# Fourier mixing in two halves of channels, and both head pairs of linear attention in one loop

## The chip, the cores and the metric

The kernel runs on one core of one Trainium2 chip. The metric is the device time of one execution in microseconds (us); the median of three runs of the kernel before is 4420.57.

## The reference

Two blocks follow each other on 2048 tokens of width 1024, all in float32. The first has two layers; each normalises and modulates the tokens (and 256 context tokens), projects them, and mixes three ways. The two ways that the change touches:

```python
def fourier_mix(u, w_four):        # u: (B, L, 256), four groups of 64 channels
    ug = u.reshape(B, L, 4, 64)
    f = jnp.fft.fft2(ug, axes=(1, 3), norm="ortho").real
    return f.reshape(B, L, 256) @ w_four

def gla_scan(q, k, v, log_a, s0):  # 4 heads, dk 48, dv 96, chunks of 64 tokens
    def step(state, inp):
        b = jnp.cumsum(gi, axis=2); b_end = b[:, :, -1:, :]
        q_dec = qi * jnp.exp(b); k_dec = ki * jnp.exp(-b)
        a = jnp.where(tri, q_dec @ k_dec.T, 0.0)
        o = a @ vi + q_dec @ state
        state = jnp.exp(b_end) * state + (ki * jnp.exp(b_end - b)).T @ vi
        return state, o
```

The scan runs forward and backward, each from the state that the context tokens leave, and the two outputs are added. The third way, neighbourhood attention with a table of biases, stands between the two. In layer 1 the context tokens need no outputs. The second block (attention, a gated MLP, embeddings) is not touched.

## The kernel before

Everything is a chain of stages. A stage is a `Block` with a program for each engine; engines wait for each other by semaphores inside it, and all meet at its end. For each layer of the first block the stages are: channel-major projection, token-major projection, Fourier (`fourier_phase`), neighbourhood attention (`neighbourhood_phase`), linear attention (`gla_phase`), output projection (`out_phase`). SP issues most DMAs from one hardware queue in program order, GpSimd ("POOL") others from its own.

**`fourier_phase`, lines 1100 to 1239.** The 2048-point transform over positions is split 128 x 16, and the transform over channels is folded with `w_four` into one 256x512 matrix `w2` (cosine and sine part). First step (L1180 to L1186): for each of 16 residues of position, and in layer 0 for the two context tiles, `ab[t] = x[t] w2`, evacuated by VectorE (L1222) and ScalarE (L1234) in turn. Second step (L1190 to L1197): for each residue four matmuls of 256 columns with the DFT table `d1` give 512 values, evacuated by ScalarE into one of four buffers `yo` (L1239) and stored by SP to the scratch `four_y` (L1141). After each of the first eight stores SP also issues six loads of bias rows (`load_near`, L1057, 48 in all). Then `four_y` is read back transposed into `ab` by four loads (L1148), which wait for all stores. Third step: for each of 16 tiles two matmuls of 256 columns with `d2` (L1205, L1206), and in layer 0 the context products with `dc` (L1210); VectorE evacuates into three buffers `fo` (L1228), GpSimd stores them (L1162, L1164) and waits for the last to land before the stage ends. The biases for the next stage are prepared here: the pad (L1031) and its copy to memory (L1035) are issued by SP, which waits for the first before it issues the lines, queries and keys (L1042 to L1047); VectorE builds the first tables (L1082, L1088) between the first step's and the third step's evacuations.

**`gla_phase`, lines 1504 to 1808.** The heads go in two pairs, `hh` 0 and 1. For each pair: the decayed keys times the decay to the chunk's end (`keys_to_end`, L1700) are transposed on TensorE and evacuated by ScalarE (L1591, L1780); batches of five chunks per direction form `k^T v` (`states`, L1613), which VectorE chains into states (`chain`, L1724: ten updates to a batch, seven batches of 35 steps); then a loop over tiles of 128 tokens, 18 in layer 0 and 16 in layer 1: scores (`products`, L1630), mask and sum of both directions (`masked`, L1734, L1737), scores times values (`inside`, L1649), queries times states (`outputs`, L1664), evacuation by ScalarE (L1789), store by SP (L1574). In each pass four batches are chained before the loop, and three in its first three tiles. The decay products of the second pair are made by VectorE in tiles 3 to 8 of the first pass (L1696, L1700, L1707), the transposes in tiles 6 and 8. Both passes share one array of states, so the second pair's chain starts after the first pass. In the second pass ScalarE and GpSimd also split the output weights into high and low parts (L1915, L1920), with the eight rows loaded by SP at its start (L1902).

```python
for hh in range(2):
    for i in range(4):
        chain(hh, i)
    for n in range(NO):
        masked(hh * NO + n)
        if n < 3:
            chain(hh, 4 + n)
        elif hh == 0:
            prepare(n - 3)
```

Of the kernel before, what the change touches and what calls it, by code (L numbers as in the profile page):

```python
# [8 lines left out]
I32 = mybir.dt.int32  # L9
# [1001 lines left out]
class Neighbourhood:  # L1011


    def __init__(self, P, last):
# [12 lines left out]
        self.lines_in, self.mask_ok, self.table_ok = P.sem("lines_in"), P.sem("mask_ok"), P.sem("table_ok")  # L1027

# [71 lines left out]
def fourier_phase(nc, l, io, keep, na):  # L1100
# [4 lines left out]
    with phase(nc, f"four{l}") as P:  # L1105
# [6 lines left out]
        dc = P.sb("dc", [128, 2, 2, 256])  # L1112
        ab = P.sb("ab", [128, N2 + 2, 512])
        yo = [P.sb(f"yo{j}", [128, 512]) for j in range(4)]
        fo = [P.sb(f"fo{j}", [128, 256]) for j in range(3)]
# [5 lines left out]
        yi_in = [P.sem(f"yi_in{j}") for j in range(4)]  # L1121
        o_out = [P.sem(f"o_out{j}") for j in range(3)]
        NAB = N2 if na.last else N2 + 2
        LF = LX if na.last else LT
        yrows = io["four_y"].rearrange("(p t) c -> p t c", t=N2)
        NO = 16 if na.last else 16 + 2
        with nc.Block() as block:
            @block.sync
            def _(sp):
# [14 lines left out]
                for j in range(4):  # L1144
                    sp.wait_ge(y_out[j], 16 * (N2 // 4))
                sp.wait_ge(y_mm, N2)
                for j in range(4):
                    sp.dma_start(ab[:, 4 * j:4 * j + 4, :],  # L1148
                                 io["four_y"][j * 512:(j + 1) * 512, :].rearrange("(a p) c -> p a c", p=128)).then_inc(yi_in[j], 16)

            @block.gpsimd
            def _(pool):
                na.clear(nc, pool)
                pool.wait_ge(na.q_in, 16)
                for i in range(3):
                    na.queries(nc, i)
                for n in range(NO):
                    pool.wait_ge(o_ev, n + 1)
                    if n < 16:

                        dst = io["mix"][0:LX, 0:256].rearrange("(a b c) d -> b a c d", a=16, b=16)[n, :, :, :]
                        pool.dma_start(dst, fo[n % 3][:, :]).then_inc(o_out[n % 3], 16)  # L1162
                    else:
                        pool.dma_start(io["mix"][LX + (n - 16) * 128:LX + (n - 15) * 128, 0:256],  # L1164
                                       fo[n % 3][:, :]).then_inc(o_out[n % 3], 16)
                for j in range(3):
                    pool.wait_ge(o_out[j], 16 * ((NO + 2 - j) // 3))

            @block.tensor
            def _(pe):  # L1170
# [9 lines left out]
                for t in range(NAB):  # L1180
# [5 lines left out]
                    last.then_inc(ab_mm, 1)  # L1186
                pe.wait_ge(d1_in, 16)
                pe.wait_ge(ab_dve, NAB // 2)
                pe.wait_ge(ab_act, NAB // 2)
                for t in range(N2):  # L1190
                    if t >= 2:
                        pe.wait_ge(y_ev, t - 1)
                    b = acc[4 + t % 2]
                    nc.tensor.matmul(b[:, 0:256], d1[:, t, 0, :], ab[:, t, 0:256], start=True, stop=False)
                    nc.tensor.matmul(b[:, 0:256], d1[:, t, 2, :], ab[:, t, 256:512], start=False, stop=True)
# [3 lines left out]
                for n in range(NO):  # L1199
                    if n >= 2:  # L1200
                        pe.wait_ge(o_ev, n - 1)
# [14 lines left out]
            def _(dve):  # L1216
# [7 lines left out]
                for n in range(NO):  # L1224
                    dve.wait_ge(o_mm, n + 1)
                    if n >= 3:
                        dve.wait_ge(o_out[n % 3], 16 * (n // 3))
# [2057 lines left out]
```

## Time and profile before

| | us |
|---|---|
| median of three runs (4420.44 to 4422.55) | 4420.57 |
| the profiled execution | 4425.12 |
| its span | 4423.3 |
| busy in it: TensorE matmuls / weight loads | 3993.2 / 3242.6 |
| busy in it: VectorE / ScalarE / GpSimd | 2073.9 / 1431.5 / 600.5 |
| mean granted TensorE clock | 0.947 |

The profile covers one execution; its span is the time from its first to its last instruction, and the sum of what the engines do can be read only against it. Matmuls are pipelined, so records of a stream overlap; the distance from start to start is what one costs. A float32 matmul has two records.

### The profile page before, as it was taken

To read this page: it belongs to the slowest core of one execution; us is meant where nothing else is said; L and a number is where in the kernel's file an instruction comes from. 1 tells how busy PE (TensorE), PEld (TensorE's weight loads), DVE (VectorE), ACT (ScalarE), POOL (GpSimd) and SP (SyncE) were. 2 spreads that over 40 slices of the span, in tenths; PEclk is the share of its full clock that TensorE was granted. 3 is DMA by queue.
4 is the path that set the end of the run, shared out by engine and by line. 5 is a ranking of instruction groups with operands and counts; after the bars stand their busy time and mean duration, and the time that the engine had idled before them with its cause. 6 is when DMAs were issued, how large, how long until landed. Compare 5 with 4: busy or idle time off the path is not lost. (4 is left out here: it accounts for less than half of the span.)

```text
span 4423.3 us, 65778 instructions
## 1 busy us (share of the span) xinstructions
PE 3993.2 (90%) x24975; PEld 3242.6 (73%) x24975; DVE 2073.9 (47%) x4599; ACT 1431.5 (32%) x3255; POOL 600.5 (14%) x669
## 2 busy tenths in 40 slices
PE   7999999799669799999979858979999989979799
PEld 4777789577558688778857647858778767768687
DVE  5364111167666542111117666732770357657554
ACT  5001344156322320144316522421111467721211
POOL 3021000033010120000012210021440001000100
PEclk8999999999779899999999979989999989979899
DMA  5244221631245432222262235441121133357221
GB/s 191 88 154 138 79 76 62 231 117 58 99 163 217 185 107 72 94 74 80 85 210 104 79 113 194 181 158 72 58 90 67 46 122 107 100 195 264 81 81 62
DMA packets 235562, 525.84 MB, mean 119 GB/s; under 512 B 55118, under 2 KB 105762, under 8 KB 225906
## 3 DMA queue, kind: packets, MB, share of 16 engines
q1 hardware_dynamic: 211634, 440.59, 28.1%
q0 software_dynamic: 23616, 81.06, 5.0%
q8 instruction: 200, 3.28, 0.3%
q14 instruction: 112, 0.92, 0.1%
HBM read 330.43 MB, written 191.13 MB: 118 GB/s over the span
## 5 line engine op out<-in xcount | busy, mean ns | idle before, releaser
L72 PE MATMUL tm_tacc<-tm_tw_hi,hT_hi 128*128 128x384 f32 (+1 forms) x1120 | 414.0, 370 | 17.9 <-DVE tm_tw_lo L906 9.6
L73 PE MATMUL tm_tacc<-tm_tw_lo,hT_hi 128*128 128x384 f32 (+1 forms) x1120 | 409.8, 366 | 0.0
L74 PE MATMUL tm_tacc<-tm_tw_hi,hT_lo 128*128 128x384 f32 (+1 forms) x1120 | 409.7, 366 | 0.0
L72 PE MATMUL tz_tacc<-tz_tw_hi,hT_hi 128*128 128x512 f32 x896 | 359.3, 401 | 5.9 <-POOL tz_tw_lo L935 3.9
L72 PE MATMUL cm_acc<-hT_hi,cm_wb_hi 128*128 128x512 f32 (+1 forms) x912 | 362.0, 397 | 0.0
L73 PE MATMUL tz_tacc<-tz_tw_lo,hT_hi 128*128 128x512 f32 x896 | 355.1, 396 | 0.0
L74 PE MATMUL tz_tacc<-tz_tw_hi,hT_lo 128*128 128x512 f32 x896 | 355.0, 396 | 0.0
L74 PE MATMUL cm_acc<-hT_hi,cm_wb_lo 128*128 128x512 f32 (+1 forms) x912 | 344.2, 377 | 0.0
L73 PE MATMUL cm_acc<-hT_lo,cm_wb_hi 128*128 128x512 f32 (+1 forms) x912 | 344.0, 377 | 0.0
L788 DVE SCALAR_TENSOR_TENSOR tm_ds<-tm_dg,tm_ds 128x512 f32<-128x512 f32 (+1 forms) x40 | 25.6, 639 | 533.2 <-ACT tm_ds L782 533.2
L72 PEld LDWEIGHTS tm_tacc<-tm_tw_hi,hT_hi 128*128 128x128 f32 x1120 | 210.6, 188 | 60.2 <-DVE tm_tw_lo L906 13.9
L74 PEld LDWEIGHTS tm_tacc<-tm_tw_hi,hT_lo 128*128 128x128 f32 x1120 | 210.8, 188 | 25.1
L73 PEld LDWEIGHTS tm_tacc<-tm_tw_lo,hT_hi 128*128 128x128 f32 x1120 | 211.0, 188 | 23.8
L72 PE MATMUL out_acc<-wo_hi,out_mT_hi 128*128 128x512 f32 x544 | 219.0, 403 | 0.0
L73 PE MATMUL out_acc<-wo_lo,out_mT_hi 128*128 128x512 f32 x544 | 215.3, 396 | 0.0
L74 PE MATMUL out_acc<-wo_hi,out_mT_lo 128*128 128x512 f32 x544 | 213.3, 392 | 0.0
L967 ACT ACTIVATE tm_tz<-tm_tacc 128x384 f32<-128x384 f32 (+1 forms) x140 | 75.6, 540 | 411.2 <-PE tm_tacc L74 410.2
L72 PEld LDWEIGHTS tz_tacc<-tz_tw_hi,hT_hi 128*128 128x128 f32 x896 | 168.9, 189 | 52.4 <-POOL tz_tw_lo L935 7.4
L704 ACT ACTIVATE cm_zo<-cm_acc 128x512 f32<-128x512 f32 (+1 forms) x57 | 32.1, 564 | 536.6 <-PE cm_acc L74 536.6
L72 PEld LDWEIGHTS cm_acc<-hT_hi,cm_wb_hi 128*128 128x128 f32 x912 | 173.3, 190 | 42.1 <-issue 12.0
L73 PEld LDWEIGHTS cm_acc<-hT_lo,cm_wb_hi 128*128 128x128 f32 x912 | 173.2, 190 | 38.0 <-issue 7.7
L74 PEld LDWEIGHTS tz_tacc<-tz_tw_hi,hT_lo 128*128 128x128 f32 x896 | 168.9, 189 | 41.1
(382 smaller groups left out, 8675.6 us busy)
## 6 DMA issues: line engine op xcount, KB each, us to landing
scr_z<-tz_tz SPq DMA_DIRECT2D x112, 256.0 KB
scr_zcm<-cm_zo SPq DMA_DIRECT2D x96, 256.0 KB, 2.0
scr_ztm<-tm_tz SPq DMA_DIRECT2D x68, 256.0 KB, 2.0
scr_xres<-out_x POOLq DMA_DIRECT2D x34, 512.0 KB, 4.1
cm_area<-in_w_ada POOLq DMA_DIRECT2D x64, 256.0 KB, 3.0
scr_z<-out_xn POOLq DMA_DIRECT2D x32, 512.0 KB, 4.7
mo_z<-scr_z SPq DMA_DIRECT2D x16, 1024.0 KB, 5.8
tz_traw<-in_w_in SPq DMA_DIRECT2D x7, 2048.0 KB, 9.1
```

The costliest lines, as they stand in the source:

```text
L72: nc.tensor.matmul(out, ah, bh, start=start, stop=False)
L73: nc.tensor.matmul(out, ah, bl, start=False, stop=False)
L74: return nc.tensor.matmul(out, al, bh, start=False, stop=stop)
L704: act.activation(zo[n % 4][:, 0:b - a], acc[n % 4][:, 0:b - a], ACT.Copy).then_inc(ev_act, 1)
L788: nc.vector.scalar_tensor_tensor(s, g, 0.0, s, ALU.min, ALU.subtract)
L967: act.activation(zo[n % 3][:, 0:widths[c]], acc[n % 3][:, 0:widths[c]], funcs[c]).then_inc(ev, 1)
```

## The change

Fourier: the second step works on one half of the channels at a time. A pass of eight units makes two residues each with 128-column matmuls; after ten of the sixteen units SP issues the first half's read-back, after the last the second's. The columns of `w2` are reordered so that each half has its cosine and sine part together. The context tiles' first and last steps move between the second and the third step. The third step fills one 512-wide bank with four tiles of a half; outputs go to one array `fo` for all tiles, stored by SP and GpSimd in turn, and their landing is waited for by SP in neighbourhood attention, at its third tile. The pad, its copy and the 48 loads of bias rows go to GpSimd's queue, ahead of its query products.

Linear attention: the second pair has its own states (in the arrays of keys and queries that are free by then, and one more). Its key products are made by GpSimd from the start, its query products by VectorE in eight pieces in tiles 3, 4, 5, 7 and 9, its transposes in tiles 3 and 4; its seven batches of states are formed after tiles 5, 7, ..., 17 and chained by VectorE one iteration later. The mask of tile g+1 goes ahead of what VectorE does for tile g. The mask itself becomes one multiplication by 0, 1 or 2 and two predicated copies of 64 columns. Values are loaded in three parts, keys scaled in five pieces, outputs have four buffers, the output weights are loaded row by row, and the high parts start at tile 3 of the second pass.

The core of the diff:

```diff
+    def four_stored(self, eng):
+        eng.wait_ge(self.four_sp, 16 * (NX // 2))
+        eng.wait_ge(self.four_pool, 16 * (NX // 2 if self.last else NT - NX // 2))
...
-                na.load_bias(sp, l, io)
                 na.load_lines(sp, io)
                 na.load_tokens(sp, io)
-                for t in range(N2):
-                    sp.wait_ge(y_ev, t + 1)
-                    sp.dma_start(yrows[:, t, :], yo[t % 4][:, :]).then_inc(y_out[t % 4], 16)
-                    if t < QR:
-                        na.load_near(sp, io, t)
...
+                for i in range(2 * NY):
+                    sp.wait_ge(y_ev, i + 1)
+                    sp.dma_start(ystore[i // NY, :, i % NY, :], yo[i % 4][:, :]).then_inc(y_out[i % 4], 16)
+                    if i == NY + 1:
+                        load_y(0)
+                load_y(1)
+                for n in range(1, NX, 2):
+                    sp.wait_ge(o_ev, first + 5 + n // 4)
+                    sp.dma_start(mix[n, :, :, :], fo[:, n, :]).then_inc(na.four_sp, 16)
...
                 na.clear(nc, pool)
+                na.load_bias(pool, l, io)
+                for r in range(QR):
+                    na.load_near(pool, io, r)
                 pool.wait_ge(na.q_in, 16)
...
+                    for x in range(2):
+                        t = 2 * u + x
+                        re, im = ab[:, t, 256 * h:256 * h + 128], ab[:, t, 256 * h + 128:256 * h + 256]
+                        b = acc[4 + i % 2][:, 256 * x:256 * x + 256]
+                        nc.tensor.matmul(b[:, 0:128], d1[:, t, 0, :], re, start=True, stop=False)
+                        nc.tensor.matmul(b[:, 0:128], d1[:, t, 2, :], im, start=False, stop=True)
+                        nc.tensor.matmul(b[:, 128:256], d1[:, t, 1, :], re, start=True, stop=False)
+                        last = nc.tensor.matmul(b[:, 128:256], d1[:, t, 0, :], im, start=False, stop=True)
...
+        build = {5 + 2 * i: i for i in range(NB)}
+        pieces = {3: (0, 1), 4: (2, 3), 5: (4, 5), 7: (6,), 9: (7,)}
...
+                masked(0)
+                for g in range(2 * NO):
+                    if g + 1 < 2 * NO:
+                        masked(g + 1)
+                    if g < 3:
+                        chain(0, 4 + g)
+                    for j in pieces.get(g, ()):
+                        queries_decayed(j)
...
+                    if g - 1 in build:
+                        chain(1, build[g - 1])
...
             def _(pool):
+                for d in range(2):
+                    pool.wait_ge(m["exp_k"], d + 1)
+                    pool.wait_ge(k_in, 16)
+                    nc.gpsimd.tensor_tensor(kd[1][d][:, :], k[:, :], kd[1][d][:, :], ALU.mult).then_inc(m["kd_ok"], 1)
...
-                    if n == KC // 2:
+                    if n == 3:
                         act.wait_ge(m["u_mm"], 2 * NB)
-                    if n < KC:
-                        wo.high(act, n)
+                    if 3 <= n < KC + 3:
+                        wo.high(act, n - 3)
```

## Rows read from the trace of the kernel before

**Rows 1.** Windows, core 0: stretch, us, busy time (instructions) by engine, granted clock, DMA.
```profile
1137.40:1276.70 139.30, 82.65 (x2072) 72.02 (x2072) 90.83 (x259) 40.69 (x106) 20.34 (x16) 0.75 0.36 126
1205.90:1218.30 12.40, 8.11 (x264) 6.80 (x264) 4.74 (x19) 2.74 (x14) 0.00 (x0) 1.00 0.19 58
1234.50:1249.00 14.50, 8.36 (x200) 7.33 (x200) 11.72 (x40) 4.00 (x9) 6.43 (x6) 0.62 0.08 25
2200.50:2313.50 113.00, 80.86 (x272) 60.54 (x272) 18.57 (x34) 14.33 (x25) 12.18 (x21) 0.91 0.67 230
2532.10:2667.90 135.80, 76.80 (x1912) 67.54 (x1912) 86.91 (x247) 38.33 (x99) 20.30 (x16) 0.75 0.36 126
```

**Rows 2.** Timeline, Fourier stage of layer 0: start, us, what [idle before, releaser].
```profile
798.52 31.24 PE L1185 MATMUL four_acc<-four_w,four_fx 128*128 128x512 f32 x72 [2.35 <-DMA four_fx<-scr_zcm]
...
830.54 0.67 PE L1194 MATMUL four_acc<-four_ab,four_d 128*128 128x256 f32 x2 [0.78 <-ACT four_ab L1234]
...
847.40 2.93 SPq L1057 DMA_DIRECT2D nain_near<-scr_rpb_pad  x6
...
863.29 3.60 DVE L1088 TENSOR_TENSOR nain_tab<-nain_near,nain_mask 128x496 f32<-128x496 f32 x6
...
867.63 0.60 ACT L1239 ACTIVATE four_yo<-four_acc 128x512 f32<-128x512 f32 x1 [1.13 <-PE four_acc L1197]
870.36 2.29 SPq L1148 DMA_DIRECT2D four_ab<-scr_four_y  x4
876.05 1.19 PE L1205 MATMUL four_acc<-four_ab,four_d 128*128 128x256 f32 x2 [8.46 <-DMA four_ab<-scr_four_y]
...
901.23 0.42 DVE L1228 COPY four_fo<-four_acc 128x256 f32<-128x256 f32 x1 [1.30 <-PE four_acc L1210]
...
906.76 0.76 PE L1347 MATMUL na_sp<-nain_k,nain_qt 64*128 64x256 f32 x1 [5.57 <-PEq L79]
```

**Rows 3.** Groups by line, whole span: count, busy, mean ns, idle before, releasers.
```profile
L1194 PE MATMUL four_acc<-four_ab,four_d 128*128 128x256 f32 x64 | 20.4, 401 | 17.7 <-ACT four_yo L1239 16.2 <-ACT four_ab L1234 1.6
L1205 PE MATMUL four_acc<-four_ab,four_d 128*128 128x256 f32 x64 | 23.0, 445 | 23.4 <-DMA four_ab<-scr_four_y 17.7 <-DVE four_fo L1228 5.4
```

**Rows 4.** Timeline, TensorE in the second block's mixing stage.
```profile
4057.21 1.05 PE L2729 MATMUL mo_SG<-mo_z,mo_wsT 128*128 128x128 f32 x8
4058.11 0.60 PE L2738 MATMUL mo_TD<-ident,mo_mx 128*128 128x128 f32 x4
```

**Rows 5.** Groups by line, GpSimd, whole span.
```profile
L1920 POOL TENSOR_TENSOR wo_lo<-wo_row,wo_hi 128x512 fp32r<-128x512 f32 x32 | 40.6, 1299 | 283.8 <-ACT wo_hi L1915 283.8
L1162 POOL DMA_DIRECT2D scr_mix<-four_fo x32 | 17.2, 536 | 124.8 <-DVE four_fo L1228 124.2 <-issue 0.7
```

**Rows 6.** Timeline, Fourier stage of layer 1, start of the second step.
```profile
2241.29 0.67 PE L1194 MATMUL four_acc<-four_ab,four_d 128*128 128x256 f32 x2 [0.78 <-ACT four_ab L1234]
```

**Rows 7.** DMA issues: count, KB each, median us to landing.
```profile
nain_k<-scr_zcm SPq DMA_DIRECT2D x2, 3456.0 KB, 18.4
```

**Rows 8.** Timeline, linear attention of layer 0.
```profile
1137.51 5.03 DVE L1700 TENSOR_TENSOR gla_kd<-nain_row,nain_eb 128x2304 f32<-128x2304 f32 x2 [3.76 <-PEq L79]
...
1149.64 4.82 PE L1613 MATMUL gla_bank<-gla_v,wo_kt 64*64 64x96 f32 x160 [2.75 <-DMA gla_v<-scr_ztm]
1151.66 13.05 DVE L1724 SCALAR_TENSOR_TENSOR gla_S<-gla_S,nain_eb,gla_bank 128x96 f32<-128x96 f32 x40 [8.63 <-PE gla_bank L1613]
...
1164.82 0.50 DVE L1734 COPY_PREDICATED gla_at<-gla_mask,gla_bank 128x128 f32<-128x128 int32 x2
1165.40 0.29 DVE L1737 TENSOR_TENSOR gla_asum<-gla_at 128x128 f32<-128x128 f32 x1
...
1191.79 4.29 PE L1591 MATMUL gla_bank<-ident,wo_ke 128*128 128x128 f32 x18
...
1220.42 13.05 DVE L1724 SCALAR_TENSOR_TENSOR gla_S<-gla_S,nain_eb,gla_bank 128x96 f32<-128x96 f32 x40 [3.89 <-PE gla_bank L1613]
...
1238.56 0.91 DVE L1737 TENSOR_TENSOR gla_asum<-gla_at 128x128 f32<-128x128 f32 x1
```

More of the change, by code:

```diff
@@ L1120, in fourier_phase @@
         y_out = [P.sem(f"y_out{j}") for j in range(4)]
[L1121 to L1126, printed above, removed]
+        yi_in = [[P.sem(f"yi_in{h}{j}") for j in range(4)] for h in range(2)]
+        NY = N2 // 2
+        ystore = io["four_y"].rearrange("(h p u) c -> h p u c", h=2, u=NY)
+        yload = io["four_y"].rearrange("(h r) (x c) -> h (r x) c", h=2, x=2)
+        first = 0 if na.last else 1
+        NO = first + 8
+        mix = io["mix"][0:LX, 0:256].rearrange("(a b c) d -> b a c d", a=16, b=16)
         with nc.Block() as block:
@@ L1179, in _, with channels @@
                 pe.wait_ge(fx_in, 16)
-                for t in range(NAB):
+                def channels(t):
                     if t >= 2:
@@ L1186, in _ @@
                     last.then_inc(ab_mm, 1)
-                pe.wait_ge(d1_in, 16)
[L1188 to L1195, printed above, removed]
-                    nc.tensor.matmul(b[:, 256:512], d1[:, t, 1, :], ab[:, t, 0:256], start=True, stop=False)
-                    nc.tensor.matmul(b[:, 256:512], d1[:, t, 0, :], ab[:, t, 256:512], start=False, stop=True).then_inc(y_mm, 1)
@@ new lines, in _ @@
+                for t in range(N2):
+                    channels(t)
+                pe.wait_ge(d1_in, 16)
+                pe.wait_ge(ab_dve, N2 // 2)
+                pe.wait_ge(ab_act, N2 // 2)
+                for i in range(2 * NY):
+                    h, u = i // NY, i % NY
+                    if i >= 2:
+                        pe.wait_ge(y_ev, i - 1)
+                    for x in range(2):
[6 more added lines that the diff above has]
+                        last = nc.tensor.matmul(b[:, 128:256], d1[:, t, 0, :], im, start=False, stop=True)
+                    last.then_inc(y_mm, 1)
@@ new lines, in _ @@
+                for j in range(8):
+                    h, b = j // 4, ready(first + j)
+                    pe.wait_ge(yi_in[h][j % 4], 16)
+                    for x in range(4):
+                        n = 4 * (j % 4) + x
+                        nc.tensor.matmul(b[:, 128 * x:128 * x + 128], d2[:, 0, :], ab[:, n, 256 * h:256 * h + 128], start=True, stop=False)
+                        last = nc.tensor.matmul(b[:, 128 * x:128 * x + 128], d2[:, 1, :], ab[:, n, 256 * h + 128:256 * h + 256], start=False, stop=True)
@@ L1514, in gla_phase @@
         mask = P.sb("mask", [128, 2, CH], I32)
+        twice, after, flat = P.sb("twice", [128, CH]), P.sb("after", [128, CH]), P.sb("flat", [128, 2, CH])
         ls = pre.ls
@@ L1691, in _ @@
+                products(0)
+                products(1)
+                for g in range(2 * NO):
+                    inside(g)
+                    if g + 2 < 2 * NO:
+                        products(g + 2)
+                    if g in QB:
+                        keys_back(1, QB.index(g))
+                    outputs(g)
+                    if g < 2:
+                        states(0, 5 + g)
+                    if g in build:
+                        states(1, build[g])
             @block.vector
@@ L1743, in _ @@
+                for d in range(2):
+                    for g in range(KG):
+                        keys_to_end(d, g)
+                nc.vector.memset(flat[:, 0, :], 0.0)
+                nc.vector.memset(flat[:, 1, :], 2.0)
+                nc.vector.memset(after[:, :], 1.0)
+                nc.vector.memset(twice[:, :], 1.0)
                 for d in range(2):
-                    nc.vector.memset(S[:, d, order[d][0], :], 0.0)
+                    nc.vector.memset(state(0, d, order[d][0]), 0.0)
```

284 lines of the change are left out of this document (149 added, 135 removed).

## The prediction

> **What bounds the kernel now.** The page first: TensorE is the busiest engine in nearly every slice, so a change pays only where TensorE itself waits. The windows by stage show where it does. Linear attention takes 139.3 us in layer 0 and 135.8 us in layer 1; in layer 0 TensorE is busy for 82.7 us of it and VectorE for 90.8 us, and the mean granted clock is 0.75 [rows 1]. It is a stage of latencies, not of one full engine. The Fourier stage of layer 1 takes 113.0 us [rows 1]. That of layer 0 begins at 786.8 us and ends with the next stage's first matmul at 906.8 us [rows 2], 120 us. Both kinds of stage end where all engines meet, so what one of them saves, the kernel saves.
>
> Then the timeline of the Fourier stage, which shows three losses. The second matmul step starts at 830.5 and its last evacuation ends at 868.2 us [rows 2], 37.7 us. Its own work is 27.8: a column costs what it costs in the first step, where 36 matmuls of 512 columns took 31.24 us [rows 2], 0.217 us for 128 columns. The rest is a stall: the stores of this step stand on SP's queue behind bias rows, 2.93 us for each six [rows 2], so ScalarE finds no free buffer. TensorE sat 16.2 us for it over the two layers [rows 3]. The second loss is the round trip through memory, from 868.2 to 876.05 us [rows 2], in which TensorE sat 17.7 us over both layers [rows 3]. The third are outputs that wait for stores out of three buffers, 5.4 us over both [rows 3], and a tail of 5.1 us between the last evacuation (901.65) and the next stage [rows 2].
>
> **Part 1, Fourier.** Layer 0. The two context tiles leave the first step: 18 tiles took 31.24 us, so 3.5 for two, and the second step starts at 827.1. It keeps its multiplications, but in 128 matmuls of 128 columns instead of 64 of 256. Is half the width at half the price? The spatial matmuls of a later stage have this very shape: 8 records, which are 4 matmuls, from 4057.21 to 4058.11 us [rows 4], 0.225 us for one. So the step takes 28.8 us and ends at 855.9, without the stall, since SP issues no bias rows now. The Trainium skill (TensorE: Matmul & The Clock Gate, LDWEIGHTS) puts a weight load of 128 columns at some 107 ns; if two loads for each matmul were not hidden, the step would grow by about 27 us a layer, an estimate by that page, and the row of the same shape speaks against it.
>
> Next the context tiles: 3.5 for the channels, 0.9 for the evacuation, 3.5 for the products, to 863.8. With the first half's third step (32 x 0.225 = 7.2, to 871.0) they cover the second half's round trip: its loads are issued at 856.8 + 2.1 = 858.9, and the first data came 5.7 us after the issue when a quarter was twice as large [rows 2], so the quarters are there from 864 to 869. TensorE ends at 878.2. Evacuation 0.9, two stores on each of two queues 1.2 (0.54 each on POOL [rows 5]), the meeting of the engines 2.1: 882.4 against 906.8. **Minus 24.4.** Only SP waits for the landing of these stores, two tiles into neighbourhood attention, where its next loads aren't urgent.
>
> Layer 1 has no context tiles. Second step from 2241.3 [rows 6] to 2270.1, first half to 2277.3. The second half's loads are issued at 2273.0, quarters land from 2277.5 to 2282.5, TensorE ends at 2285.5, and 4.2 as above: 2289.7 against 2313.5. **Minus 23.8.**
>
> Moved to GpSimd's queue: the load of the pad, its copy to memory, 48 row loads. The trace has no POOL issue of so many short runs. One of 128 runs of 1 KB takes 0.54 us [rows 5]; the row loads have 256 runs each. Floor 0.54, ceiling 1.07, and I take 0.6, the row they are nearest to. Pad and copy should be done at about 802: two round trips of some 5 us, where today the pad's load sits in SP's own ring behind 6 MB. The 48 end at 832, or at 853 by the ceiling. VectorE then needs 3.6 us for six tables [rows 2] and 0.6 for the mask, and is next asked for at 858 in layer 0, later in layer 1. Cost nothing, at either end. SP's loads of queries and keys move up by 18 us. The keys take 18.4 us to land [rows 7]; now they follow the DFT tables, and the first y stores, from 828.5, may queue behind them: 0 to 5 us a layer. I take 0, since all 14 MB have 40 us by then and landed in about that.
>
> **Part 2, linear attention,** layer 0, in us after the stage's start at 1137.4. Today the values, one load of 3.5 MB, hold the first state matmuls until 12.2, and VectorE's chain starts at 14.3 [rows 8]. Now 8 of 18 tiles come first, and the keys are scaled in pieces of 0.6 us instead of two of 2.5 [rows 8]. What is late next is ten groups of transposes with their evacuations, until 8.5. The chain starts at 10.5: four batches of 3.26 (40 updates took 13.05 [rows 8]) and 0.5 for the new masks, the first tile's mask at 24.1 instead of 27.4. Three tiles with a batch each took 14.5 us in today's second pass [rows 1]: to 39.
>
> The keys' four products leave VectorE for GpSimd. Its price is 1.30 us for 512 columns [rows 5], so 5.8 for 2304. At the rate of today's values load, the first decay row and the keys are there at 14, the second row and its exponential at 24.5, so the two pairs of products end at 25.5 and 37, and are needed at 39 and 45. At 1.5 times that price the second would be 4 late. Tiles 3 and 4 carry the transposes (4.3 us for half of them [rows 8]), 6.2 us each; the query pieces lie beside these. Tile 5 and the first batch of the second pair's state matmuls: 54.
>
> Then seven rounds of two tiles and one batch. VectorE: ten updates 3.26 and two masks. A mask today is 0.50, a gap of 0.08, 0.29 and a gap of 0.1 to 0.2 [rows 8]; the new one multiplies 128 elements and copies twice 64, 0.95. Round: 5.2. TensorE is busy 1.16 us a tile (8.11 us for seven in 12.40 us [rows 1]) and 1.2 for 40 records of a batch (4.82 for 160 [rows 8]), 3.5 in all, hidden. Today's tiles take 1.77 [rows 1]. The seventh batch ends at 54 + 31.2 + 3.3 = 88.5, at tile 18. The chain of 13.05 us that today starts the second pass [rows 8] and the three slow tiles behind it are gone. What is left ends by GpSimd's low halves, 16 x 1.30 = 20.8 [rows 5], from the first high half at 93 to 114, or by the 15 tiles of ScalarE, about as late; plus 2.5: 116.5 against 139.3. **Minus 22.8.** Layer 1 has two tiles fewer before the high halves: low halves from 90 to 111, stage 113.3 against 135.8. **Minus 22.5.** Output stores had two buffers and get four; that is in it.
>
> Sum: 24.4 + 23.8 + 22.8 + 22.5 = 93.5. The profiled execution took 4425.1 us (span 4423.3), so 4331.6; the median of the runs lies 4.5 below it: **4327 us**.
>
> **A rule against the overlap.** Today a VectorE sum of two SBUF operands takes 0.91 us beside a GpSimd product and 0.29 without [rows 8]. The Trainium skill (SBUF — State Buffer, Who interferes with whom) says that such a pair shuts each other out for a whole instruction. Here a query piece that meets one of the 5.8 us products would wait it out. By the sum GpSimd is done 2 us before the first piece; if it is not, up to 12 us over both layers come back, which is the smaller form of rival B.
>
> **Rivals.**
> A (0.55): as summed, 4327, own range 4312 to 4342.
> B (0.20), slow rounds. Today three tiles with batches ran at a mean clock of 0.62, TensorE busy 8.4 of 14.5 us, while 8.1 of 12.4 kept 1.00 [rows 1]; 3.5 of 5.2 lies beside the second, which speaks against B. At 1.2 GHz TensorE needs up to 7.0 a round, so rounds lie between 5.2 and 7.0; at 6.4 fourteen of them cost 17: 4344.
> C (0.17), queues in Fourier: y stores behind the keys, or row loads that delay both. Then the second step stalls about as today, half of part 1 goes: 4351.
> D (0.04), the other side: GpSimd's issue grows with short runs. At x us for each of the 48, VectorE gets them at 802 + 48x and 853 is free; at x = 2.1 the excess of 50 a layer eats the whole gain, and beyond it the kernel is slower: at 2.5 it is 69 a layer, 4327 + 138 = 4465. Against it: that is four times the nearest row [rows 5]. For it: the trace has no issue of such runs there.
> E (0.04): the new order of linear attention gains nothing, since VectorE's work is only moved and the rounds give back the chain: 4327 + 45 = 4372.
>
> **Numbers.** The range takes A with its terms, B and C: 4308 to 4360; it leaves out D, E and what is worse than C. About 0.2%, 9 us, is what a measurement here can tell from no change. Faster: A, B, C, and E less a little, 0.95; same 0.02; slower 0.03.
>
> **What would show it.** Right: no idle of TensorE by ScalarE's y buffers, the first half's loads issued inside the second step, the next stages at about 882 and 24 us earlier again in layer 1, tables built before 858, linear attention of 116 and 113 us with seven rounds of 5.2 and no chain between the passes. Wrong: 128-column matmuls that step by 0.4 us, tables after 858, rounds of 6 or more, transposes of the second pair that wait for GpSimd.

## The result and the profile after

The changed kernel takes **4341.1 us** (median of four runs, 4340.5 to 4342.7) against 4421.6 (4420.4 to 4423.2) for the kernel before, run beside it: a ratio of 0.9818, 95% interval 0.9801 to 0.9835. That is 80.4 us less. The forecast was 4327, so 14 us of the expected gain are missing.

First the windows of the four changed stages in the profile after. A row gives the stretch, us, the busy time of TensorE, its weight loads, VectorE, ScalarE and GpSimd, the granted clock, the DMA share and GB/s. In order: Fourier of layer 0, linear attention of layer 0, the stretch of its rounds, Fourier and linear attention of layer 1.

```profile
786.46:890.04 103.58, 85.16 (x488) 70.46 (x488) 18.72 (x28) 14.91 (x25) 37.40 (x64) 0.93 0.81 260
1120.99:1238.48 117.49, 74.18 (x2072) 66.48 (x2072) 71.69 (x276) 40.30 (x106) 37.92 (x20) 0.82 0.43 150
1174.50:1210.50 36.00, 23.59 (x891) 21.02 (x884) 28.80 (x117) 5.88 (x30) 0.00 (x0) 0.99 0.25 77
2160.99:2256.72 95.73, 77.14 (x464) 66.25 (x464) 17.32 (x26) 14.29 (x24) 36.24 (x63) 0.93 0.85 272
2475.58:2588.00 112.42, 69.69 (x1912) 61.89 (x1912) 68.56 (x264) 38.37 (x98) 37.91 (x20) 0.83 0.44 152
```

Against [rows 1] and, for the first stage, [rows 2], that is

| stage | before | forecast | after | saved (forecast) |
|---|---|---|---|---|
| Fourier, layer 0 | 119.8 | 95.6 | 103.6 | 16.2 (24.4) |
| linear attention, layer 0 | 139.3 | 116.5 | 117.5 | 21.8 (22.8) |
| Fourier, layer 1 | 112.9 | 89.2 | 95.7 | 17.2 (23.8) |
| linear attention, layer 1 | 135.8 | 113.3 | 112.4 | 23.4 (22.5) |
| the rest | 3915.5 | same | 3909.5 | 6.0 (0) |

Linear attention came out as summed, 45.2 against 45.3 us. Fourier gave 33.4 instead of 48.2: here the sum missed (the two stages are 8.0 and 6.5 us longer than forecast, 14.5). Of the 6.0 us in the rest, 4.7 lie behind the last changed stage, in identical code. The profiled execution of before was 4.5 us longer than the median that the forecast starts from; that of after is 0.6 shorter than its own. So the profiles differ by 84.6 us in span, 8.9 short of the 93.5 that were summed, while the median misses its forecast by 14.1: the 6.0 us that nobody forecast and the 5.1 by which the two profiled executions lie differently against their medians nearly cancel. That the miss of the median is as large as that of the Fourier stages is therefore partly chance.

The timeline of Fourier, layer 0, after (start, us, engine and line, what [idle before, releaser]):

```profile
799.85 1.65 PE L1201 MATMUL four_acc<-four_w,four_fx 128*128 128x512 f32 x2 [3.99 <-DMA four_fx<-scr_zcm]
...
804.35 26.63 POOL L1062 DMA_DIRECT2D nain_near<-scr_rpb_pad  x48 [12.09 <-DMA scr_rpb_pad<-nain_pad]
...
805.81 1.70 SPq L1052 DMA_DIRECT2D nain_k<-scr_zcm  x1
...
830.13 0.46 PE L1222 MATMUL four_acc<-four_ab,four_d 128*128 128x128 f32 x2 [0.78 <-ACT four_ab L1278]
...
841.00 0.60 ACT L1283 ACTIVATE four_yo<-four_acc 128x512 f32<-128x512 f32 x1 [2.85 <-DMA scr_four_y<-four_yo]
...
850.35 2.09 SPq L1154 DMA_DIRECT2D four_ab<-scr_four_y  x4
...
859.73 1.18 ACT L1283 ACTIVATE four_yo<-four_acc 128x512 f32<-128x512 f32 x2 [2.89 <-DMA scr_four_y<-four_yo]
...
863.04 2.02 SPq L1154 DMA_DIRECT2D four_ab<-scr_four_y  x4
...
882.02 0.69 DVE L1271 COPY four_fo<-four_acc 128x512 f32<-128x512 f32 x1 [1.09 <-PE four_acc L1247]
...
883.00 1.08 POOL L1182 DMA_DIRECT2D scr_mix<-four_fo  x2 [0.73 <-DVE four_fo L1271]
...
890.04 0.74 POOL L1373 MEMSET na_tab<- 128x768 f32 x1 [5.96 <-POOLq L79]
```

What to see: the round trip that cost 8.46 us of idle TensorE in [rows 2] is gone, since the first half's read-back (850.35) lies inside the second step and the second half's (863.04) behind other work. The stall by bias rows is gone too: the 48 are issued by GpSimd in 26.6 us. What is left is small but adds up. The first step starts 1.7 us later after the stage's start than before. ScalarE waits for a free buffer twice, 2.85 and 2.89 us where its usual gap is 1.19. And 7.3 us pass between the end of the last evacuation (882.7) and the next stage's first work (890.04), with GpSimd idle for 5.96 of them; before it was 4.9 (901.65 to GpSimd's first work at 906.57; the 5.1 of the prediction run to the first matmul, 906.76 [rows 2]).

The groups of the second step, both layers, after. They answer to [rows 3].

```profile
L1222 PE MATMUL four_acc<-four_ab,four_d 128*128 128x128 f32 x128 | 25.1, 278 | 3.9 <-ACT four_yo L1283 2.4 <-ACT four_ab L1278 1.6
L1246 PE MATMUL four_acc<-four_ab,four_d 128*128 128x128 f32 x128 | 24.8, 276 | 1.4 <-DMA four_ab<-scr_four_y 1.4
```

TensorE's idle time by ScalarE's buffers fell from 16.2 to 2.4 us, and by read-backs from 17.7 to 1.4.

Linear attention of layer 0, after, VectorE and GpSimd:

```profile
1131.33 3.17 DVE L1785 SCALAR_TENSOR_TENSOR gla_S<-gla_S,nain_eb,gla_bank 128x96 f32<-128x96 f32 x10 [4.21 <-PE gla_bank L1685]
...
1142.96 3.17 DVE L1785 SCALAR_TENSOR_TENSOR gla_S<-gla_S,nain_eb,gla_score 128x96 f32<-128x96 f32 x10 [4.89 <-PE gla_score L1685]
...
1149.70 0.29 DVE L1794 TENSOR_TENSOR gla_asum<-gla_score,gla_twice 128x128 f32<-128x128 f32 x1
...
1151.27 4.05 POOL L1840 TENSOR_TENSOR wo_ke<-gla_kd,nain_eb 128x2304 f32<-128x2304 f32 x1
...
1175.90 3.17 DVE L1785 SCALAR_TENSOR_TENSOR gla_k<-gla_k,nain_eb,gla_bank 128x96 f32<-128x96 f32 x10 [0.48 <-PE gla_bank L1685]
...
1199.45 0.29 DVE L1794 TENSOR_TENSOR gla_asum<-gla_score,gla_twice 128x128 f32<-128x128 f32 x1 [0.19 <-issue]
...
1204.08 0.29 DVE L1794 TENSOR_TENSOR gla_asum<-gla_score,gla_twice 128x128 f32<-128x128 f32 x1 [0.19 <-issue]
...
1205.60 3.17 DVE L1785 SCALAR_TENSOR_TENSOR gla_q<-gla_q,nain_eb,gla_bank 128x96 f32<-128x96 f32 x10
```

The chain starts 10.3 us into the stage (forecast 10.5). Its third batch waits 4.89 us, which the prediction did not have: TensorE sits for 8.5 us before it by the third part of the values. The first mask is at 28.7 us (24.1), but the first batch of the second pair at 54.9 (54), and the seventh ends at 87.8 (88.5). One round (a batch and two masks) is 4.63 us (1199.45 to 1204.08; forecast 5.2), at a granted clock of 0.99; the first rounds, which also hold query pieces and waits, take up to 5.67.

### The profile page after: what moved, and what is told of

Same layout as the page of the kernel before. It is cut to its first block and busy times, and to the rows that moved or that the text cites. A ratio compares the mean times of both kernels' runs of the same rounds, so it can differ in the third digit from the quotient of the medians.

```text
span 4338.7 us, 66488 instructions
## 1 busy us (share of the span) xinstructions
PE 3965.7 (91%) x25359; PEld 3237.6 (75%) x25359; DVE 2034.2 (47%) x4616; ACT 1432.1 (33%) x3255; POOL 684.0 (16%) x761
## 5 line engine op out<-in xcount | busy, mean ns | idle before, releaser
L73 PEld LDWEIGHTS tm_tacc<-tm_tw_lo,hT_hi 128*128 128x128 f32 x1120 | 211.1, 189 | 23.8
L704 ACT ACTIVATE cm_zo<-cm_acc 128x512 f32<-128x512 f32 (+1 forms) x57 | 32.2, 565 | 536.1 <-PE cm_acc L74 536.1
```

The lines of the kernel that those rows point to most:

```text
L73: nc.tensor.matmul(out, ah, bl, start=False, stop=False)
L704: act.activation(zo[n % 4][:, 0:b - a], acc[n % 4][:, 0:b - a], ACT.Copy).then_inc(ev_act, 1)
```

## The experiments

Theory: the forecast's mechanisms hold, and the missing 14.5 us of Fourier are three things left out of the sum: GpSimd's queue holds the stage's end, the keys delay the stores of the second step, and the read-back delays the last of them. The rivals are bandwidth, the copy of the pad, and the two parts acting on each other.

### e1 and e2: each part alone

e1 has the changed Fourier stage (the diff's parts up to neighbourhood attention) and the old linear attention; e2 the reverse.

> Linear attention as before, the Fourier stage as changed. The changed kernel's profile gives the Fourier stages 103.5 and 95.7 us against 119.9 and 113.0, so 33.7 saved where the prediction had 48.2. If the two parts are independent: 4421.6 - 33.7 = 4388 us, and the Fourier stages of the profile within 1 us of 103.5 and 95.7, linear attention at 139 and 136. If the parts act on each other (for example a queue left busy by one stage in the next), the stages differ from these by several us.

Measured: 4386.4 us against 4419.1, ratio 0.9921 (0.9906 to 0.9936). Fourier 101.2 and 94.1 us, linear attention 139.5 and 134.1.

> The Fourier stage as before, linear attention as changed. The changed kernel's profile gives 117.5 and 112.4 us against 139.3 and 135.8, so 45.2 saved, the prediction had 45.3. If the parts are independent: 4421.6 - 45.2 = 4376 us, stages of 117.5 and 112.4, Fourier at 120 and 113. Otherwise the stages differ from these by several us.

Measured: 4368.0 us against 4419.1, ratio 0.9882 (0.9867 to 0.9897). Linear attention 115.5 and 110.3, Fourier 119.0 and 111.3.

The parts save 32.7 and 51.1 us, together 83.8 where both at once save 80.4. In this and the later profiles the stages of one code differ from execution to execution: the changed Fourier stage by up to 2.7 us (100.9 to 103.6 in layer 0), the changed linear attention by up to 4.6 (115.5 to 119.9, and 110.4 to 115.0). So this is independence as far as it can be told, and a stage's length in one profile says little about an edit worth less than that; the waits inside it say more.

### e3: output stores without GpSimd

The loop goes from GpSimd's program to the end of ScalarE's.

```diff
-                for n in range(0, NX, 2):
-                    pool.wait_ge(o_ev, first + 5 + n // 4)
-                    pool.dma_start(mix[n, :, :, :], fo[:, n, :]).then_inc(na.four_pool, 16)
+                for n in range(0, NX, 2):
+                    act.wait_ge(o_ev, first + 5 + n // 4)
+                    act.dma_start(mix[n, :, :, :], fo[:, n, :]).then_inc(na.four_act, 16)
```

> The changed kernel, with the eight even output stores of each Fourier stage issued by ScalarE, which is idle there, instead of GpSimd. Theory 1, GpSimd's queue holds the meeting of the engines until its last stores have been carried out: the tail from the last evacuation to the next stage falls from 7.3 and 7.1 us to about 3.3 (two issues of 0.6 and 2.1 for the meeting), 8 us less in all, 4333. Theory 2, the stores themselves or the meeting of all engines take that long whichever queue issues them: tails of 7, 4341.

Measured: 4334.9 us against 4419.1, ratio 0.9805 (0.9789 to 0.9822). The end of Fourier, layer 0, in this run:

```profile
878.89 6.79 ACTq L1288 DMA_DIRECT2D scr_mix<-four_fo  x8
...
878.89 6.52 SPq L1167 DMA_DIRECT2D scr_mix<-four_fo  x8
...
883.53 0.69 DVE L1270 COPY four_fo<-four_acc 128x512 f32<-128x512 f32 x1 [1.09 <-PE four_acc L1246]
...
887.00 0.06 DVE L1509 MEMSET nain_ls<- 128x1 f32 x1 [2.78 <-PEq L79]
```

From the last evacuation's end (884.2) to GpSimd's first work (886.93) are 2.7 us, and 2.7 in layer 1, where the changed kernel had 7.3 and 7.0. **Theory 1 holds** for the tails; the time is 6.2 us below the changed kernel's, with intervals that overlap. SyncE and ScalarE issue their last stores as late and leave at once: ScalarE's last store is issued by 885.68 and lands some 2 us later, after the next stage has begun. GpSimd, with the same stores, is the last to come to the meeting. That the code no longer waits for these stores there does not help while they are on its queue. In layer 0 the stage is only 3.0 us shorter than the changed kernel's, because in this execution the second step stood longer for its stores (34.8 us from its first matmul to its last evacuation's end, against 30.8).

### e4: the keys behind the read-backs

The load of `load_tokens` becomes a function of its own, called later.

```diff
-        eng.dma_start(self.kk[:, :, :], io["zcm"][5:8, :, :].rearrange("c p t -> p c t")).then_inc(self.k_in, 16)
...
                 load_y(1)
+                na.load_keys(sp, io)
```

> The changed kernel, with the keys of neighbourhood attention (3.4 MB) loaded on SyncE's queue behind the second half's read-back instead of ahead of the first store of the second step. Theory 1, the stores of the second step wait in the queue behind the keys (they land 32 us after their issue here): ScalarE's waits for a free buffer in the middle of the step (2.9 us in layer 0, 4.1 in layer 1) go, the step takes 28.6 us, 3 to 5 us a layer are saved if the keys land before the next stage begins, about 25 us after their issue: 4333. Theory 2, the stores wait for bandwidth taken by the row loads or by the first half's read-back: the waits stay, and the time is 4341 or, if the keys are late for the next stage, longer.

Measured: 4340.7 us against 4419.1, ratio 0.9819 (0.9805 to 0.9834), the time of the changed kernel. The time alone would say that the theory fell. The profile says something else: in the middle of the second step ScalarE's gaps are 1.19 us throughout in both layers, and the last evacuation of layer 1 ends at 85.4 us of the stage, not 88.7. Of these 3.3 us the second step gives 1.7 (30.3 us, not 31.9); 1.2 are an earlier start of the step, which the edit doesn't explain. DMA issues (count, KB each, median us to landing), the changed kernel first, then e4:

```profile
nain_k<-scr_zcm SPq DMA_DIRECT2D x2, 3456.0 KB, 32.1
nain_near<-scr_rpb_pad POOLq DMA_DIRECT2D x96, 32.0 KB, 13.4
```

```profile
nain_k<-scr_zcm SPq DMA_DIRECT2D x2, 3456.0 KB, 15.9
nain_near<-scr_rpb_pad POOLq DMA_DIRECT2D x96, 32.0 KB, 7.3
```

Then the end of layer 1's stage in e4:

```profile
2244.30 0.69 DVE L1274 COPY four_fo<-four_acc 128x512 f32<-128x512 f32 x1 [1.09 <-PE four_acc L1250]
...
2245.28 1.05 POOL L1185 DMA_DIRECT2D scr_mix<-four_fo  x2 [0.73 <-DVE four_fo L1274]
...
2255.87 0.74 POOL L1376 MEMSET na_tab<- 128x768 f32 x1 [9.53 <-POOLq L79]
```

All 3.3 us are given back: GpSimd now sits for 9.53 us after its last issue (5.70 in the changed kernel's layer 1), because its stores land behind the keys; its last one lands 6.3 us after GpSimd's last issue is done, against 2.5. A repair was eaten by the wait that e3 removes.

### e5: the second step's stores on ScalarE's queue

```diff
                     act.activation(yo[i % 4][:, :], acc[4 + i % 2][:, :], ACT.Copy).then_inc(y_ev, 1)
+                    act.wait_ge(y_ev, i + 1)
+                    act.dma_start(ystore[i // NY, :, i % NY, :], yo[i % 4][:, :]).then_inc(y_out[i % 4], 16)
```

> The changed kernel, with the 16 stores of the second step issued by ScalarE behind each of its evacuations, so that SyncE's queue holds neither the keys nor the first half's read-back ahead of them. Theory 1, order in the queue: both of ScalarE's waits for a free buffer go, the one in the middle (1.7 us above the usual gap in layer 0, 2.9 in layer 1) and the one at the end (1.7 in both); the second half's read-back starts earlier and its wait of 1.6 us in layer 1 shrinks: 7 to 10 us less, 4333. ScalarE has 1.19 us idle in each unit of 1.79 to issue in. Theory 2, bandwidth: the DMA engines are busy for 0.8 of the stage, so stores in a queue of their own are as slow: waits stay, 4341, or longer by the issues on ScalarE.

Measured: 4338.9 us against 4420.6, ratio 0.9811 (0.9794 to 0.9829). In layer 0:

```profile
837.75 0.60 ACT L1279 ACTIVATE four_yo<-four_acc 128x512 f32<-128x512 f32 x1 [4.09 <-DMA scr_four_y<-four_yo]
...
855.73 0.60 ACT L1279 ACTIVATE four_yo<-four_acc 128x512 f32<-128x512 f32 x1 [2.14 <-DMA scr_four_y<-four_yo]
```

The wait in the middle stays (4.09, and 3.94 in layer 1), so it is not the order on SyncE's queue: the keys delay these stores also from another queue. The one at the end shrinks, from 2.89 to 2.14 us. That is theory 2 for the first wait and half of theory 1 for the second. The Trainium skill (DMA: Bandwidth & Descriptors, Queues, rings and completion order) says that each of the 16 DMA engines takes turns between the queues that have work for it, so a queue of its own does not make a transfer free; these rows agree with it.

### e6: all values first

```diff
                 load_values(1)
+                load_values(2)
                 sp.dma_start(qd[1][0][:, :], decay_sums(io, 1, 0)).then_inc(b_in[0], 16)
                 sp.dma_start(k[:, :], io["zcm"][11, :, :]).then_inc(k_in, 16)
-                load_values(2)
```

> The changed kernel, with the third part of the values (1.9 MB) of linear attention loaded ahead of the decay row and the keys of the second pair instead of behind them. Theory 1: VectorE's chain waits 4.9 us in each layer for state products that wait for these values; 2.3 MB fewer are ahead of them, 5.5 us at the 0.42 MB/us seen there, so the wait goes, 4.5 to 4.9 us a layer are saved, and GpSimd's products, 4.6 us later, still end about 5 us before TensorE needs them: 4332. Theory 2: what GpSimd loses is on the path to the transposes of the second pair, and the gain is given back at the fourth and fifth tile: 4341.

Measured: 4331.5 us against 4420.6, ratio 0.9795 (0.9780 to 0.9811), the largest gain of one edit. Linear attention takes 111.6 and 109.2 us instead of 117.5 and 112.4; the third batch follows the second without a wait. These lengths lie below all of those with the old order of loads (115.5 to 119.9 and 110.4 to 115.0), and so do those of e9, e10 and e11, which have this edit too. GpSimd's products end 39.5 us into the stage instead of 34.3 and TensorE does not wait for them; one query piece of layer 1 met their end and took 1.16 us instead of 0.68. **Theory 1 holds.**

### e7: the copy of the pad behind the Fourier inputs

```diff
         eng.wait_ge(self.pad_in, 16)
+        eng.wait_ge(fx_in, 16)
```

> The changed kernel, with GpSimd's copy of the bias pad to memory held until the Fourier inputs have landed. Theory 1: the copy, in runs of 192 bytes, takes DMA time from these inputs, which land 12.4 us after their issue against 10.7 before the change, so the first step starts 1.3 us late and its second tile later still; held, the first step starts as before, 2 to 3 us a layer less if the copy and the row loads that follow are not needed sooner: 4337. Theory 2: the inputs are late for another reason, the time stays at 4341, tables about 5 us later and still hidden.

Measured: 4339.8 us, ratio 0.9820 (0.9802 to 0.9837), no difference. The first evacuation of layer 0 comes 14.4 us into the stage, against 16.8 in the changed kernel and 13.8 before; but the kernels that keep the copy where it is have it anywhere from 13.0 (e5) to 16.6 (e4), and e2, with the Fourier stage of before, at 14.6. So the late start in the profile after is mostly a variation from execution to execution, whose cause stays open; one profile can't say that the copy has no part in it. In e7's layer 1 the second step took 36.5 us, with a wait of ScalarE of 6.02 us, the longest of all profiles with the row loads on GpSimd's queue; whether the held copy did that, the run doesn't show.

### e8: bias rows back on SyncE's queue

The same calls leave GpSimd's program.

```diff
+                na.load_bias(sp, l, io)
                 na.load_lines(sp, io)
...
                     sp.dma_start(ystore[i // NY, :, i % NY, :], yo[i % 4][:, :]).then_inc(y_out[i % 4], 16)
+                    if i < QR:
+                        na.load_near(sp, io, i)
```

> Undoes one part: halves of channels and everything else as changed, but the bias pad, its copy and the 48 row loads back on SyncE's queue, six behind each of the first eight stores of the second step. If the order on SyncE's queue was what cost the second step its 8 us a layer, the step stalls again: eight stores with six row loads each need 8 x (2.9 + 0.6) = 28 us where eight units of TensorE take 14.3, so 10 to 14 us a layer come back, less about 3 that the row loads cost now elsewhere (late inputs, late keys): 4341 + 14 to 22, 4358. If the gain came from the halves alone: 4341.

Measured: 4355.8 us against 4420.6, ratio 0.9856 (0.9840 to 0.9871). Fourier takes 108.1 and 106.4 us. SyncE's queue:

```profile
834.73 0.45 SPq L1160 DMA_DIRECT2D scr_four_y<-four_yo  x1
...
835.22 2.93 SPq L1062 DMA_DIRECT2D nain_near<-scr_rpb_pad  x6
...
838.20 0.45 SPq L1160 DMA_DIRECT2D scr_four_y<-four_yo  x1
```

A store every 3.47 us where TensorE needs 1.79 for its unit. So of the 33.4 us that Fourier saves, all but the move brings 18.2 (119.8 + 112.9 - 108.1 - 106.4), and the move to GpSimd's queue, on top of it, 15.2. The 15.2 are a balance. The second step is 25.7 us shorter by the move over both layers (30.8 and 31.9 us instead of 43.5 and 44.9; it was 37.7 and 38.7 before the change, where no first half was read back inside it). But other things are worse with the move. In e8 the keys land in 18.3 us, not 32.1, so it is the row loads beside them that slow them. And the tail is 5.3 and 5.1 us in e8, not 7.3 and 7.0, though GpSimd issues the same output stores:

```profile
887.69 1.05 POOL L1182 DMA_DIRECT2D scr_mix<-four_fo  x2 [0.73 <-DVE four_fo L1271]
892.73 0.74 POOL L1373 MEMSET na_tab<- 128x768 f32 x1 [3.99 <-POOLq L79]
```

GpSimd sits for 3.99 us here where it sat for 5.96, so 2 us of each tail come with the 50 bias DMAs on GpSimd's queue, the last of which had landed at 842.9 in the changed kernel. Why they still count at the stage's end no run shows; e3 removes them too.

### e9, e10 and e11: the repairs together

e9 is e3, e4 and e6 in one. e10 adds e5. e11 adds to e10 that GpSimd's queue loads the weight rows and that VectorE makes every second low half:

```diff
-                    if NO <= g < NO + KC:
-                        wo.load_row(sp, l, io, g - NO)
...
+                pool.wait_ge(m["o_ok"], NO)
+                for j in range(KC):
+                    wo.load_row(pool, l, io, j)
+                for j in range(0, 2 * KC, 2):
+                    wo.low(nc, pool, j)
...
+                    if 0 <= g - NO - 6 < KC:
+                        wo.low(nc, dve, 2 * (g - NO - 6) + 1)
```

> The changed kernel with three edits together: even output stores of Fourier on ScalarE's queue, neighbourhood keys behind the read-backs, values of linear attention ahead of the second pair's rows. If the three mechanisms are separate, the tails of the Fourier stages are 2.7 us in both layers (the keys no longer delay stores that GpSimd waits for), the wait in the middle of the second step is gone, and linear attention takes 112 and 109 us: Fourier 101.1 - 4.6 - 1.1 = 96 and 94.6 - 4.3 - 3.3 = 87 us, so 4331.5 - 12 = 4319 us. If the keys land too late for the next stage, its first tiles wait and up to 5 us a layer come back: 4328.

Measured: 4321.5 us against 4421.3, ratio 0.9773 (0.9758 to 0.9787). Fourier 95.5 and 88.7 us, linear attention 111.8 and 108.4, each within 2 us of what was expected. The keys are late for layer 1's next stage, which takes 222.0 us instead of 218.9:

```profile
2237.72 0.79 PE L1400 MATMUL na_sp<-nain_k,nain_qt 64*128 64x256 f32 x1 [6.03 <-DMA nain_k<-scr_zcm]
```

> The kernel of e9, with the 16 stores of the second step on ScalarE's queue too. With the keys out of the way, what is left of ScalarE's waits is the one at the end of the step (1.7 us a layer), behind the first half's read-back. If order on SyncE's queue makes it, it goes: 2 to 3 us less than e9 in all. If the read-back takes the bandwidth, it stays, as half of it did in e5: 0 to 1 us less.

Measured: **4318.7 us**, ratio 0.9769 (0.9754 to 0.9783). The wait at the end of the step, 2.96 us in e9's layer 0 and 4.39 in its layer 1, is gone (1.2 and 1.4). The 2.8 us are within what the intervals leave open; the gaps are not. The step's length over all profiles tells the same, from its first matmul to its last evacuation's end: 30.7 to 36.5 us, 32.2 in the mean, in the 14 stages with the keys ahead (the changed kernel, e1, e3, e5, e6, e7, e12), 30.0 to 31.4 with the keys behind (e4, e9), 29.5 in all four with the stores on ScalarE's queue as well (e10, e11).

> The kernel of e10, with the eight weight rows at the end of linear attention loaded on GpSimd's queue, not between the output stores on SyncE's, and half of the 16 low halves given to VectorE. Theory 1: ScalarE's waits for a free output buffer and for rows (5.7 us of idle VectorE in layer 0, 3.0 + 1.8 + 2.2 in layer 1) come from the order on SyncE's queue, and GpSimd's 19.7 us of low halves would bound the stage next; with both gone 3 to 5 us a layer are saved: e10 less 8. Theory 2: 6 MB of rows and the stores share bandwidth, or VectorE's and GpSimd's low halves, both from SBUF to SBUF, shut each other out (the pair of a sum and a product took 0.91 against 0.29 us before the change): e10 within 2 us, or slower.

Measured: 4319.6 us, ratio 0.9769 (0.9753 to 0.9785): nothing gained, the time of theory 2. The low halves by engine, both layers (count, ns least/median/most, first and last start):

```profile
L2007 POOL TENSOR_TENSOR wo_lo<-wo_row,wo_hi x16: 1256/1574/1728, 1201.8 to 2553.7; 128x512 fp32r<-128x512 f32 x16
L2007 DVE TENSOR_TENSOR wo_lo<-wo_row,wo_hi x16: 683/1130/1540, 1202.5 to 2556.2; 128x512 fp32r<-128x512 f32 x16
```

Beside each other both are slower: VectorE's median is 1.13 us with 0.68 as the least, GpSimd's 1.57 where it was 1.27 alone in the changed kernel. ScalarE waits for no row any more and still waits for stores in layer 0, for up to 2.23 us; so the first half of theory 1 came true in part and won nothing that the time shows.

### e12: query pieces beside GpSimd's products

```diff
-        pieces = {3: (0, 1), 4: (2, 3), 5: (4, 5), 7: (6,), 9: (7,)}
+        pieces = {4: (2, 3), 5: (4, 5), 7: (6,), 9: (7,)}
...
+                    if g == 0:
+                        queries_decayed(0)
+                        queries_decayed(1)
```

> The changed kernel, with the first two of VectorE's query pieces (0.7 us each, SBUF to SBUF) moved from the fourth tile to the first, where GpSimd's products of 4.1 and 5.1 us are running (1151.3 to 1155.3 and 2500.0 to 2509.2 us in the changed kernel's profile; the pieces would start at 1151.0 and 2504.7). Theory 1, the two engines shut each other out for a whole instruction: the first or second piece waits for a product to end, 3 to 5 us in each layer, the chain behind it begins that much later, and the stages grow by 3 to 4 us: 4341 + 7 = 4348. Theory 2, they share: each piece takes 0.7 to 1.2 us (1.16 was the longest so far, beside a product's end), the stages grow by 0 to 1 us, 4341 to 4343.

Measured: 4347.1 us against 4420.3, ratio 0.9838 (0.9821 to 0.9854). Layer 0:

```profile
1147.32 5.35 DVE L1777 TENSOR_TENSOR gla_qd<-gla_q,gla_qd 128x576 f32<-128x576 f32 x2
...
1152.59 3.16 DVE L1785 SCALAR_TENSOR_TENSOR gla_S<-gla_S,nain_eb,gla_bank 128x96 f32<-128x96 f32 x10
```

```profile
1147.61 4.44 POOL L1843 TENSOR_TENSOR wo_ke<-gla_kd,nain_eb 128x2304 f32<-128x2304 f32 x1
```

The pair of pieces takes 5.35 us instead of 1.42. The longest single one took 4.60: it ends 0.6 us after GpSimd's product does (1152.05). **Theory 1 holds**, and the same in layer 1 (5.38 us). The chain's updates, which have one operand in PSUM, took 0.31 us each (median) beside a product and without. That agrees with the Trainium skill (SBUF — State Buffer, Who interferes with whom), by which a VectorE instruction with two SBUF inputs contends with a GpSimd instruction that reads SBUF, and one with at most one such input does not contend with GpSimd.

## Why the prediction was right and where it was wrong

The direction and the range were right, and rival A was the case that came, with a sum 14 us too good, at the very edge of A's own range (4341.1 of 4342), and there partly by the chance told above: the rest of the kernel gave 6.0 us that were not in the sum, and the 4.5 us that were taken off because one profiled execution lay above its median did not come back in the profile after. By the prediction's own steps:

**Halves at half the price: right.** The units of eight 128-column matmuls come every 1.787 us, 0.223 for one (forecast 0.225); the 27 us a layer that the prediction put on weight loads that aren't hidden did not come.

**The second step without a stall: wrong, a term too small.** It ends 74.5 us into layer 0's stage (forecast 70.0) and 73.1 into layer 1's (70.5). The text named the cause, "the first y stores, from 828.5, may queue behind them: 0 to 5 us a layer. I take 0". The reason for the 0 was the error: 14 MB in 40 us, as before. But the row loads now run at the same time as the keys, in short runs, and the keys land 32.1 us after their issue, not 18.4 [rows 7]; in e8, with the rows elsewhere, it is 18.3. e4 shows it from the other side: without the keys there, no wait. The first half's read-back adds a second wait of 1.7 us a layer, which the sum did not have at all; e10 removes it. ScalarE catches up a part of each wait (the gap behind the first is 0.50 us, not 1.19), so together they lengthen the step by 3.3 us over both layers (30.8 and 31.9 us, forecast 29.7 each). The second step's late start (43.7 and 41.2 us into the stages, forecast 40.3 and 40.8), mostly the variation seen in e7, is another 3.7.

**The round trip behind other work: right.** 1.4 us of waiting left, expected 1.0.

**The tail: wrong, the largest term.** The prediction allowed 3.3 us behind the last evacuation; it was 7.3 and 7.0, in all 7.8 us of the 14.5 (3.3 and 3.7 are above, and the third step is 0.3 faster than summed). It said "Only SP waits for the landing of these stores". No instruction waits, yet GpSimd's queue does (e3), and some 2 us of each tail come with the bias loads that were moved to the same queue (e8). The trace of before could have told the first: its tail of 5.1 us was read as a wait for a landing that the change removes. e3 has 2.7.

**The bias loads on GpSimd: right for the issues, wrong in "Cost nothing, at either end".** 0.555 us an issue, between the floor of 0.54 and the 0.6 taken; the rows are there at 842.9 (853 allowed) and the tables done at 847.3 (858). But the loads delay the keys, and with them the stores, and they lengthen the tail (e8). Rival D was far off, and rival C (queues) came in its small form.

**Linear attention: right in sum, by two errors that cancel.** The values' third part cost 4.9 us at the third batch and was not in the sum (e6). Against it, from the first pair's last batch to the second pair's first, past the transposes, it took 11.3 us instead of 15, and the six rounds between the seven batches took 4.62 to 5.67 us, mean 4.95, instead of 5.2 (layer 1: mean 4.88): the new mask costs 0.64 us a tile, not 0.95. What ended the stage was as forecast: GpSimd's 16 low halves, to 113.4 us (forecast 114), and ScalarE's last tile, to 114.7. Rival B did not occur: the rounds ran at a clock of 0.99.

**The rule against the overlap: not met here, and true.** GpSimd was done 10 us before the first query piece, not 2: its products took 5.05 and 4.05 us, not 5.8. e12 forces the meeting, and a piece waits out a product.

## What to carry to other kernels

A meeting of engines can be held by a queue that no instruction waits for. In this kernel it was GpSimd's: output stores issued by it cost 4.5 us a stage that the same stores from SyncE or ScalarE, also still in flight, did not (e3), and 2 of the 4.5 only came with many short loads issued earlier on the same queue (e8). When a transfer is moved to an idle queue, price what it then runs beside, not only what it no longer stands before: and look at the next wait, too, for the later keys brought nothing alone (e4), while with the stores off GpSimd's queue Fourier was 8.1 and 7.0 us shorter (e9), against 3.0 and 5.7 for the stores alone (e3, whose 3.0 holds a second step that took 4 us longer in that execution). And before a load is put first for one consumer, look which consumer waits first: exchanging two loads gave 9.6 us in the medians.

## What the runs showed of the hardware

- With output stores on GpSimd's queue the next stage began 5.96 us after GpSimd's last issue, 9.53 where 3.4 MB were in flight ahead of them (e4), 3.99 where the 50 bias DMAs were not on this queue (e8). From the last evacuation to the next stage it was 7.3 us in the changed kernel and 2.7 with the stores on ScalarE's queue (e3).
- Stores on SyncE's and ScalarE's queues did not hold the end: in e3 the next stage began at 886.93, 1.25 us after the last issue, with a store that takes 2.9 us to land.
- A queue of its own did not shield 256 KB stores from 3.4 MB in another (e5: waits of 4.09 and 3.94 us).
- 96 loads in short runs on GpSimd's queue took 13.4 us to land beside the keys and 7.3 without, and the keys 32.1 beside them, 18.3 in e8 with the rows on SyncE's queue behind them.
- A product of two SBUF operands on VectorE of 0.75 us took 4.60 beside a GpSimd product (e12); differences of two SBUF operands took 0.68 us at least and 1.13 in the median beside GpSimd's, which grew from 1.27 to 1.57 (e11).
- The first evacuation of one Fourier stage (layer 0) lay between 13.0 and 16.8 us after its start in kernels that do the same up to there. No run here tells why.
